# Two edits to a three-part FP32 transformer trunk at once: high and low x in one matmul, and another order of the mixer's steps

## The chip, the cores and the metric

One core of a Trainium2 chip. The metric is the device time of one execution in microseconds (us). The kernel before takes 1033.99 us, the median of three runs (1033.08 to 1035.55). TensorE has two clock levels here, 2.4 GHz (granted clock 1.00 in the profile) and 1.2 GHz (0.50).

## What is computed

Two layers over x of 256 tokens by 1024 features, in FP32. Each layer has a half-step FFN, a mixer of three head groups, and a second half-step FFN, each with a residual and a LayerNorm behind it.

```python
def swiglu(x, w_gate, w_up, w_down):
    return (jax.nn.silu(x @ w_gate) * (x @ w_up)) @ w_down

for l in range(DEPTH):
    x = layer_norm(ALPHA * x + 0.5 * swiglu(x, ffn1_w_gate[l], ffn1_w_up[l], ffn1_w_down[l]), ...)
    x = layer_norm(ALPHA * x + hybrid_mixer(x, ...), ...)
    x = layer_norm(ALPHA * x + 0.5 * swiglu(x, ffn2_w_gate[l], ffn2_w_up[l], ffn2_w_down[l]), ...)
```

The hidden width is 2816. The mixer makes one input product x @ w_in and feeds three groups with it: a gated recurrence (RG-LRU) behind a causal convolution, attention of six heads with a forget gate, and a state-space group (S5) with a GELU and a gate. Their outputs go through a root-mean-square norm each and one output product.

## The kernel before, in words

**Precision.** TensorE takes FP32 in one rounded pass (type fp32r). To keep the precision, every large operand is kept as a high part (rounded) and a low part (what rounding left). A product is three matmuls: high by high, high by low, low by high. `mm3` (lines 1605 to 1609) issues them. For features (`features`, line 1627, and the later `z_event`s) the weights are the stationary operand, in tiles of 128 x 128, and x, transposed, is the moving one, 256 columns. For the down product the moving operand is 512 columns of weights.

**Pieces.** Weights come in 157 pieces of 128 x 2048 through a ring of five slots (`RING`). A piece is loaded by SyncE once the piece five before is used (`pieces_used`), ScalarE copies it to its high part (`split_hi`, line 689), VectorE subtracts for the low part (`split_lo`, line 1072). Each engine's order is written out by hand; `ahead(n)` stands where an engine splits piece n.

**An FFN** (TensorE: `ffn`, line 1748) runs over 11 pairs q of 256 hidden features. A pair has a gate piece, an up piece and a down piece. Pair 0 has the tokens as output rows (`first_pair`), and its product is turned by four transposes. For pairs 1 to 10 TensorE does gate(q), up(q), down(q-1); pass q is this triple. The last three down products come at the end, in halves. Gate goes to PSUM bank 4, up to bank 6, each 512 wide: two tiles of features side by side, 256 tokens each. The down product accumulates in banks 0 to 3 over the whole FFN. Behind a pair stand, in this order: SiLU on ScalarE (`silu_pair`, line 725), the product with up on VectorE (`hidden`, line 1101), the high part on ScalarE (`hidden_hi`, line 730), the low part on VectorE (`hidden_lo`, line 1110). Gate(q) waits for SiLU(q-1), up(q) for the product of q-1. The product of the first pair is taken from banks 4 to 7, its second token tile from banks 4 and 5 (`TOK_BANKS`, `hidden_rows`, line 1086).

**Tables.** Beside the first FFN of a layer the parameters of the mixer are turned and worked out: `turn(parR)`, `outputs_turned` (in the code before part of `ffn`), `inputs_turned`, `responses` on TensorE, with copies on ScalarE and VectorE, and powers on GpSimd (lines 556 to 637). They use banks 5 and 7, which are free of FFN work in the passes.

**The mixer** (VectorE lines 1537 to 1594, ScalarE 960 to 1037, TensorE 1993 to 2050, GpSimd 642 to 672). TensorE's input products are `z_event(0)` to `z_event(17)`. Between them stand the S5 inputs, the forget sums, the S5 outputs (`s5_outputs`, line 1852, waits for VectorE's last rotation, line 1440), the gates of the recurrence, and for each head scores, transposed probabilities and values. A head goes: `scores` (TensorE), `attn_logits` (VectorE), `attn_exp` (ScalarE), `attn_recip` (VectorE), `attn_scale` (GpSimd, line 645), `turn_probs` (TensorE). Between the S5 outputs and the GLU product the S5 result is put from block order into token order: a GELU on ScalarE (`s5_gelu`, line 879) into `gin`, then 16 small copies by VectorE (`blocks_out`, line 1500) into `gs`. TensorE's order around the two edits is

```python
s5_outputs(); gates(1); scores(0); scores(1); z_event(12); gates(2); z_event(13)
turn_probs(0); glu(); scores(2); scores(3); turn_probs(1); z_event(14)
```

Of the kernel before, what the change touches and what calls it, by code (L numbers as in the profile page):

```python
# [106 lines left out]
RG_V_OM = 1  # L107
RG_V_GATED = 7
# [6 lines left out]
def trunk(nc, x, w, out):  # L115
    ctx = ExitStack()
    with ctx:
# [15 lines left out]
        xT_hi = sb("xT_hi", [P, KD, SEQ], F32R)  # L133
        xT_lo = sb("xT_lo", [P, KD, SEQ], F32R)
# [76 lines left out]

        def qpad(h):
            return qf[:, h, :] if h < 4 else qT[:, h - 4, :]
# [37 lines left out]
        hi_done = sem("hi_done")  # L251
        lo_done = sem("lo_done")
# [53 lines left out]
        def used(L, pos):  # L306

            return L * LAYER_N + pos + 1

# [158 lines left out]
        def _(pool):  # L468
# [28 lines left out]
            for L in range(DEPTH):  # L497
# [164 lines left out]

                attn_scale(0)
# [22 lines left out]
        def _(act):  # L686
# [20 lines left out]
            for L in range(DEPTH):  # L707
# [17 lines left out]
                def silu_pair(f, q):  # L725

                    act.wait_ge(pieces_used, used(L, gate_pos(f, q)))
                    A.activation(silu, bank[4][:, :], ACT.Silu).then_inc(ly.silu_done, 1)  # L728
# [13 lines left out]

                def ffn(f):
# [7 lines left out]
                    for q in range(1, PAIRS - 2):  # L751
                        if q == 2 and f == 0:
                            exponentials()
                            outputs_in()
# [3 lines left out]
                        ahead(base + gate_pos(f, q + 1))  # L758
                        ahead(base + up_pos(f, q + 1))
                        hidden_hi(f, q)  # L760
                        if q < PAIRS - 3:
                            ahead(base + down_pos(f, q))
                    silu_pair(f, PAIRS - 2)
                    if f == 0:
                        inputs_in(0)
                    ahead(base + gate_pos(f, PAIRS - 1))
                    ahead(base + up_pos(f, PAIRS - 1))
                    hidden_hi(f, PAIRS - 2)
                    if f == 0:
                        inputs_in(2)  # L770
                    ahead(base + down_pos(f, PAIRS - 3))
                    silu_pair(f, PAIRS - 1)
                    ahead(base + down_pos(f, PAIRS - 2))
                    if f == 0:
                        responses_in()
                    ahead(base + down_pos(f, PAIRS - 1))
                    if f == 0:
                        responses()
# [7 lines left out]
                def outputs_in():  # L786

                    act.wait_ge(c_turned, L + 1)
                    for r in range(2):
                        A.activation(cpow[:, r, :, 0, :], bank[7][:, r * SEQ:(r + 1) * SEQ], ACT.Copy)\  # L790
                            .then_inc(cpow_ready, 1)

                def inputs_in(first):

                    for n in (first, first + 1):
                        act.wait_ge(b_turned, 4 * L + n + 1)
                        A.activation(bst[:, n // 2, 4 * (n % 2):4 * (n % 2) + 4, :], bank[5 + 2 * (n % 2)][:, :], ACT.Copy)\
                            .then_inc(bst_ready, 1)

                def responses_in():  # L800

                    for n in range(2):
                        act.wait_ge(k_summed, 2 * L + n + 1)
                        A.activation(ksb[:, 4 * n:4 * n + 4, :], bank[5 + 2 * n][0:CH, :], ACT.Copy).then_inc(k_evac, 1)
# [186 lines left out]
                ahead_mix(8)  # L991
                attn_exp(0)
                attn_exp(1)
                query_out(12, 1)
# [56 lines left out]
        def _(vec):  # L1051
# [25 lines left out]
            for L in range(DEPTH):  # L1077
# [23 lines left out]
                def hidden(f, q):  # L1101

                    vec.wait_ge(ly.silu_done, silu_count(f, q))
                    vec.wait_ge(pieces_used, used(L, up_pos(f, q)))
                    vec.wait_ge(ly.hid_lo, PAIRS * f + q)
                    if q == 1:
                        vec.wait_ge(ly.hid_turned, f + 1)
                    V.tensor_tensor(hid, silu, bank[6][:, :], ALU.mult).then_inc(ly.hid_done, 1)  # L1108
# [8 lines left out]
                def ffn(f):  # L1117
# [7 lines left out]
                    for q in range(1, PAIRS - 2):  # L1125
                        if q == 1 and f == 0:
                            spread_steps()
                        elif q == 2 and f == 0:
                            angles()
                        ahead(base + gate_pos(f, q + 1))  # L1130
                        ahead(base + up_pos(f, q + 1))
                        hidden(f, q)
                        if q == 2 and f == 0:
                            softplus()
                        hidden_lo(f, q)
                        if q < PAIRS - 3:
# [4 lines left out]
                    ahead(base + up_pos(f, PAIRS - 1))  # L1141
                    hidden(f, PAIRS - 2)
                    hidden_lo(f, PAIRS - 2)
                    ahead(base + down_pos(f, PAIRS - 3))
                    ahead(base + down_pos(f, PAIRS - 2))
                    if f == 0:
                        skip_terms()
# [53 lines left out]
                def angles():  # L1201
# [872 lines left out]
```

## Time and profile before

| | |
|---|---|
| median of three runs | 1033.99 us (1033.08 to 1035.55) |
| profiled execution | 1034.52 us |
| its span, first to last instruction | 1032.8 us |
| TensorE matmuls | busy 97%, 6982 |
| TensorE weight loads | busy 90%, 6982 |
| VectorE | busy 62% |
| ScalarE | busy 48% |
| GpSimd | busy 31% |
| mean granted TensorE clock | 0.983 |
| DMA | 176.68 MB, mean 171 GB/s |

Times in the trace are microseconds from the span's start. A matmul's row shows its start, and its end is modelled: matmuls overlap, so the pace is read from start to start. The square brackets at a row's end give the engine's idle time before it and who ended it.

### The profile page before, as it was taken

How to read it: one execution, taken by the hardware profiler on the slowest of the kernel's cores; microseconds unless marked ns; L12 is line 12 of the kernel's file. 1: busy time of each engine (PE TensorE's matmuls, PEld its weight loads, DVE VectorE, ACT ScalarE, POOL GpSimd, SP SyncE). 2: the span in 40 equal slices, each digit the busy share in tenths (PEclk: the TensorE clock that was granted, in tenths of full speed). 3: DMA queues.
4: the chain of work that ended last, by engine and by line, in shares of the span. 5: the costliest groups of instructions: out<-in, count | busy, mean ns of one | idle time of the engine just before them, and what ended most of it. 6: DMA issues, size and time to landing. Idle time of an engine off the chain costs nothing.

```text
span 1032.8 us, 16441 instructions
## 1 busy us (share of the span) xinstructions
PE 997.9 (97%) x6982; PEld 934.5 (90%) x6982; DVE 639.7 (62%) x756; ACT 493.1 (48%) x602; POOL 320.1 (31%) x382
## 2 busy tenths in 40 slices
PE   7999999999899999999999999999999999999997
PEld 6999999898788999999899999998988889999995
DVE  4674644788687744444787664457787876545446
ACT  4553433647774443433555434264668544343441
POOL 3039991051230700000062699700703334000000
PEclk9999999999899999999999999999979999999998
DMA  9755565374144656565486656545622357555541
GB/s 299 231 193 179 189 189 178 120 195 135 42 134 152 226 182 196 173 202 168 158 234 205 201 168 202 176 151 164 164 82 82 123 171 237 175 193 186 182 164 41
DMA packets 142392, 176.68 MB, mean 171 GB/s; under 512 B 11312, under 2 KB 126704, under 8 KB 142320
## 3 DMA queue, kind: packets, MB, share of 16 engines
q1 hardware_dynamic: 140592, 169.35, 51.7%
q0 software_dynamic: 1728, 6.29, 1.6%
q8 instruction: 55, 0.90, 0.4%
q14 instruction: 17, 0.14, 0.0%
HBM read 174.56 MB, written 1.05 MB: 170 GB/s over the span
## 4 chain that ended last, share of the span: by engine, by line
PE 87%; DVE 8%; ACT 2%; issue 1%; DMA 1%; POOL 1%; SPq 0%; DVEq 0%
PE bank L1607 27%; PE bank L1608 27%; PE bank L1609 27%; PE bank L1612 2%; DVE wlo L1074 1%; DVE gs L1507 1%; ACT u L876 1%; ACT whi L692 1%; PE bank L1742 1%; PE bank L1932 1%; DVE xT_f L1317 1%; PE bank L1860 1%; DMA xtok<-in_x 1%; PE bank L1891 1%; DVE xa L1397 1%
## 5 line engine op out<-in xcount | busy, mean ns | idle before, releaser
L1074 DVE TENSOR_TENSOR wlo<-raw,whi 128x2048 fp32r<-128x2048 f32 (+1 forms) x157 | 387.6, 2490 | 286.8 <-ACT whi L692 286.4
L1607 PE MATMUL bank<-xT_hi,whi 128*128 128x256 f32 x1504 | 429.0, 285 | 0.0
L1609 PE MATMUL bank<-xT_hi,wlo 128*128 128x256 f32 x1504 | 425.6, 283 | 0.0
L1608 PE MATMUL bank<-xT_lo,whi 128*128 128x256 f32 x1504 | 425.6, 283 | 0.0
L692 ACT ACTIVATE whi<-raw 128x2048 fp32r<-128x2048 f32 (+1 forms) x157 | 293.4, 1895 | 12.6 <-DMA raw<-in_ffn_w_up 4.8
L1607 PEld LDWEIGHTS bank<-xT_hi,whi 128*128 128x128 f32 x1504 | 288.5, 192 | 3.4 <-issue 1.7
L1608 PEld LDWEIGHTS bank<-xT_lo,whi 128*128 128x128 f32 x1504 | 288.5, 192 | 1.3
L1609 PEld LDWEIGHTS bank<-xT_hi,wlo 128*128 128x128 f32 x1504 | 288.4, 192 | 0.0
L1607 PE MATMUL bank<-whi,act_hi 128*128 128x512 f32 x376 | 147.6, 393 | 0.0
L1608 PE MATMUL bank<-wlo,act_hi 128*128 128x512 f32 x376 | 146.8, 391 | 0.0
L1609 PE MATMUL bank<-whi,act_lo 128*128 128x512 f32 x376 | 146.5, 390 | 0.0
L527 POOL TENSOR_TENSOR xtok<-xn,lngb 128x1024 f32<-128x1024 f32 x10 | 32.3, 3228 | 336.7 <-DVE xT_lo L1349 336.7
L728 ACT ACTIVATE gs<-bank 128x512 f32<-128x512 f32 x40 | 23.9, 597 | 209.6 <-PE bank L1609 209.5
L740 ACT ACTIVATE act_hi<-uT 128x512 fp32r<-128x512 f32 x36 | 22.8, 632 | 130.4 <-DVE uT L1108 130.4
L1609 PEld LDWEIGHTS bank<-whi,act_lo 128*128 128x128 f32 x376 | 70.6, 188 | 15.1
L1607 PEld LDWEIGHTS bank<-whi,act_hi 128*128 128x128 f32 x376 | 70.8, 188 | 13.7
L1608 PEld LDWEIGHTS bank<-wlo,act_hi 128*128 128x128 f32 x376 | 70.8, 188 | 13.2
L1607 PE MATMUL bank<-whi,xT_hi 128*128 128x256 f32 (+1 forms) x192 | 58.4, 304 | 10.3 <-DVE xT_lo L1349 9.4
L1609 PE MATMUL bank<-whi,xT_lo 128*128 128x256 f32 (+1 forms) x192 | 57.4, 299 | 0.0
L1608 PE MATMUL bank<-wlo,xT_hi 128*128 128x256 f32 (+1 forms) x192 | 57.3, 298 | 0.0
L1607 PEld LDWEIGHTS bank<-whi,xT_hi 128*128 128x128 f32 x192 | 40.3, 210 | 11.7 <-DVE xT_lo L1349 10.3
L1114 DVE TENSOR_TENSOR act_lo<-uT,act_hi 128x512 fp32r<-128x512 f32 x36 | 26.1, 726 | 23.8 <-ACT act_hi L740 23.8
(309 smaller groups left out, 1066.2 us busy)
## 6 DMA issues: line engine op xcount, KB each, us to landing
raw<-in_ffn_w_up SPq DMA_DIRECT2D x44, 1024.0 KB, 5.4
raw<-in_ffn_w_down SPq DMA_DIRECT2D x44, 1024.0 KB, 5.0
raw<-in_ffn_w_gate SPq DMA_DIRECT2D x43, 1024.0 KB, 5.4
raw<-in_w_in SPq DMA_DIRECT2D x12, 1024.0 KB, 5.3
raw<-in_w_out SPq DMA_DIRECT2D x8, 1024.0 KB, 5.4
raw<-in_w_in SPq DMA_DIRECT2D x12, 512.0 KB, 5.3
lngb<-in_ln_g POOLq DMA_DIRECT2D x6, 512.0 KB, 5.8
lngb<-in_ln_b POOLq DMA_DIRECT2D x6, 512.0 KB, 6.8
```

Source lines behind the costliest of these rows:

```text
L527: mark_x(pool.tensor_tensor(xtok[:, t, :], xn[:, t, :], lngb[:, 0, :], ALU.mult))
L692: A.activation(piece(whi, n, 8, PC)[:, :, cols], piece(raw, n, 8, PC)[:, :, cols], ACT.Copy).then_inc(hi_done, 1)
L728: A.activation(silu, bank[4][:, :], ACT.Silu).then_inc(ly.silu_done, 1)
L740: A.activation(hid_tiles(q)[0], src.rearrange("p (a n) -> p a n", a=2), ACT.Copy)\
L876: A.activation(u4[b * CH:(b + 1) * CH, i::4, 1:], src[i * CH:(i + 1) * CH, :, :, b], ACT.Copy)\
L1074: V.tensor_tensor(piece(wlo, n, 8, PC)[:, :, cols], piece(raw, n, 8, PC)[:, :, cols], piece(whi, n, 8, PC)[:, :, cols].bitcast(F32), ALU.s ...
L1114: V.tensor_tensor(lo, src.rearrange("p (a n) -> p a n", a=2), hi.bitcast(F32), ALU.subtract)\
L1317: lnstep(V.tensor_scalar(xT_f[:, 1, k, :], bank[LN_BANKS[n][t][1]][:, k * P:(k + 1) * P], prow(g0, 4 + k), prow(b0, 4 + k), ALU.mult, ALU. ...
L1607: T.matmul(out, a_hi, b_hi, start=first, stop=False)
L1608: T.matmul(out, a_hi, b_lo, start=False, stop=False)
L1609: return T.matmul(out, a_lo, b_hi, start=False, stop=last)
L1612: return T.transpose(dst, src, ident[:, :])
```

## The change

Two edits, put in together.

**x side by side.** `xT_hi` and `xT_lo` become two halves of one tile, `xT[P, KD, 2, SEQ]`. `features` issues, for each of eight row tiles k, one matmul of the high weights with 512 columns (high x and low x) and one of the low weights with high x, 256 columns. Each feature tile gets a bank of its own: gate 4 and 5, up 6 and 7. In a bank, columns 0 to 255 hold high·high + low·high, columns 256 to 511 high·low. ScalarE copies the upper halves to SBUF (`low_part`), VectorE adds the lower halves (`gate_sums`, and at the head of `hidden`), SiLU and the product then work on SBUF. Gate(q) and up(q) wait for these sums of q-1. The table work that used banks 5 and 7 moves to places between passes where gate's banks 4 and 5 are free. `z_event` and `rows` keep three matmuls.

```diff
-        xT_hi = sb("xT_hi", [P, KD, SEQ], F32R)
-        xT_lo = sb("xT_lo", [P, KD, SEQ], F32R)
+        xT = sb("xT", [P, KD, 2, SEQ], F32R)
+        xT_hi, xT_lo = xT[:, :, 0, :], xT[:, :, 1, :]
...
-                def features(n, bnk):
+                def features(n, bnk, second=None):
...
                     for ft in range(2):
+                        if ft and second:
+                            pe.wait_ge(*second)
                         for k in range(KD):
                             c = slice(ft * P, (ft + 1) * P)
-                            ins = mm3(bank[bnk][:, ft * SEQ:(ft + 1) * SEQ], hi[:, k, c], lo[:, k, c],
-                                      xT_hi[:, k, :], xT_lo[:, k, :], k == 0, k == KD - 1)
+                            T.matmul(bank[bnk + ft][:, :], hi[:, k, c], xT[:, k, :, :].rearrange("p a n -> p (a n)"),
+                                     start=k == 0, stop=False)
+                            ins = T.matmul(bank[bnk + ft][:, 0:SEQ], lo[:, k, c], xT_hi[:, k, :], start=False,
+                                           stop=k == KD - 1)
...
+                    if q == 1:
+                        pe.wait_ge(ly.silu_done, silu_count(f, 0))
+                        features(base + gate_pos(f, q), 4, (ly.hid_done, silu_count(f, 0)))
+                    else:
+                        pe.wait_ge(parts_added, gate_sums_done(L, f, q - 1))
+                        features(base + gate_pos(f, q), 4)
...
+                def low_part(f, q, first, dst):
...
+                    A.activation(dst.rearrange("p (a n) -> p a n", a=2), banks[:, first:first + 2, SEQ:], ACT.Copy)\
+                        .then_inc(low_copied, 1)
...
                 def hidden(f, q):
 
+                    both = hid.rearrange("p (a n) -> p a n", a=2)
+                    vec.wait_ge(low_copied, up_sums_done(L, f, q))
+                    V.tensor_tensor(both, banks[:, 6:8, 0:SEQ], both, ALU.add).then_inc(parts_added, 1)
+                    vec.wait_ge(parts_added, up_sums_done(L, f, q))
                     vec.wait_ge(ly.silu_done, silu_count(f, q))
...
+                    V.tensor_tensor(hid, silu, hid, ALU.mult).then_inc(ly.hid_done, 1)
+
+                def gate_sums(f, q):
+
+                    both = silu.rearrange("p (a n) -> p a n", a=2)
+                    vec.wait_ge(low_copied, gate_sums_done(L, f, q))
+                    V.tensor_tensor(both, banks[:, 4:6, 0:SEQ], both, ALU.add).then_inc(parts_added, 1)
```

TensorE's first FFN of a layer: the parameters are turned after gate sum 1 and gate(2) waits until VectorE has copied them (`parameters_in`, behind the product of pass 1); the output tables are turned after up(2), the input tables after up(6) and up(7), the responses after up(8) (`MATS = 6`).

**The mixer's order.**

```diff
@@ GpSimd
+                pool.wait_ge(y_gelu, L + 1)
+                for i in (2, 3):
+                    block_moves(pool, i)
+                pool.wait_ge(ys_gelu, 16 * L + 16)
                 attn_scale(0)
@@ ScalarE
-                ahead_mix(8)
                 attn_exp(0)
                 attn_exp(1)
+                ahead_mix(8)
                 query_out(12, 1)
@@ VectorE
                 ahead_mix(2)
-                ahead_mix(3)
                 forget_log()
                 forget_series()
+                conv(0)
+                ahead_mix(3)
                 s5_turn_back()
-                conv(0)
                 s5_scans()
...
                 ahead_mix(5)
-                blocks_out()
                 attn_logits(0)
                 attn_logits(1)
-                ahead_mix(6)
+                blocks_out()
                 attn_recip(0)
                 attn_recip(1)
-
+                ahead_mix(6)
                 ahead_mix(7)
```

`block_moves(engine, i)` is four of the 16 small copies; VectorE's `blocks_out` keeps i = 0 and 1, GpSimd takes 2 and 3.

## Rows read from the trace of the kernel before

**Rows 1.** The page, busy time, share of the span and instructions.
```profile
PE 997.9 (97%) x6982; PEld 934.5 (90%) x6982; DVE 639.7 (62%) x756; ACT 493.1 (48%) x602; POOL 320.1 (31%) x382
```

**Rows 2.** TensorE's waits: waiter, releaser, us in total, times, longest.
```profile
PE bank L1607 <- DVE xT_lo L1349: 9.4, 5, 2.0
```

**Rows 3.** Timeline, one pass of layer 0's second FFN: start, us, engine, instruction.
```profile
374.95 0.28 PE L1607 MATMUL bank<-xT_hi,whi 128*128 128x256 f32 x1
...
386.46 0.40 PE L1607 MATMUL bank<-whi,act_hi 128*128 128x512 f32 x1
...
391.93 0.28 PE L1607 MATMUL bank<-xT_hi,whi 128*128 128x256 f32 x1
```

**Rows 4.** The same pass: busy us per engine, then SiLU and VectorE's product.
```profile
374.95:391.93 16.98, 16.98 (x122) 16.02 (x120) 8.07 (x6) 6.64 (x5) 0.00 (x0) 1.00 0.58 186
...
380.90 0.60 ACT L728 ACTIVATE gs<-bank 128x512 f32<-128x512 f32 x1 [6.99 <-PE bank L1609]
387.74 0.68 DVE L1108 TENSOR_TENSOR uT<-gs,bank 128x512 f32<-128x512 f32 x1
```

**Rows 5.** Timeline, starts of layer 1's FFNs: gate product 1 and VectorE.
```profile
531.69 0.28 PE L1607 MATMUL bank<-xT_hi,whi 128*128 128x256 f32 x1
534.84 0.41 DVE L1098 TENSOR_TENSOR uT<-gs,bank 128x256 f32<-128x256 f32 x1
...
849.54 0.28 PE L1607 MATMUL bank<-xT_hi,whi 128*128 128x256 f32 x1
853.54 0.41 DVE L1098 TENSOR_TENSOR uT<-gs,bank 128x256 f32<-128x256 f32 x1
```

**Rows 6.** Timeline of TensorE in the mixers of layer 0 and layer 1.
```profile
253.24 0.43 PE L1858 MATMUL bank<-u,kst 128*128 128x64 f32 x2 [1.97 <-DVE xn L1440]
...
272.16 0.90 PE L1612 MATMUL bank<-ident,lngb 128*128 128x128 f32 x3 [4.52 <-POOL lngb L650]
...
278.00 0.36 PE L1607 MATMUL bank<-xT_hi,whi 128*128 128x256 f32 x1
...
760.82 0.43 PE L1858 MATMUL bank<-u,kst 128*128 128x64 f32 x2 [1.97 <-DVE xn L1440]
...
783.33 0.55 PE L1612 MATMUL bank<-ident,lngb 128*128 128x128 f32 x3 [1.54 <-POOL lngb L650]
...
787.00 0.36 PE L1607 MATMUL bank<-xT_hi,whi 128*128 128x256 f32 x1
```

**Rows 7.** Timeline of VectorE, layer 0's mixer: a weight split, the 16 block moves.
```profile
236.74 2.29 DVE L1074 TENSOR_TENSOR wlo<-raw,whi 128x2048 fp32r<-128x2048 f32 x1 [3.84 <-ACT whi L692]
...
260.38 4.88 DVE L1507 COPY gs<-gin 32x128 f32<-32x128 f32 x16
```

**Rows 8.** Timeline of ScalarE, layer 0's mixer.
```profile
234.69 0.21 ACT L969 ACTIVATE fx<-fx 128x12 f32<-128x12 f32 x1
...
258.85 0.60 ACT L882 ACTIVATE gin<-bank 128x512 f32<-128x512 f32 x1 [0.84 <-PE bank L1860]
...
262.19 1.91 ACT L692 ACTIVATE whi<-raw 128x2048 fp32r<-128x2048 f32 x1
...
266.18 0.40 ACT L945 ACTIVATE lngb<-lngb,nmx 128x128 f32<-128x128 f32 x1 [0.77 <-DVE nmx L1520]
...
268.73 0.77 ACT L895 ACTIVATE kpad<-bank 64x256 f32<-64x256 f32 x2
```

**Rows 9.** Timeline of GpSimd, layer 0's mixer: the first head's scaling, the second's first.
```profile
269.26 2.39 POOL L648 TENSOR_SCALAR lngb<-lngb,rrec 128x128 f32<-128x128 f32 x1 [33.31 <-DVE rrec L1524]
271.63 0.47 POOL L650 TENSOR_SCALAR lngb<-lngb,rrec 128x256 f32<-128x256 f32 x1
272.08 0.37 POOL L648 TENSOR_SCALAR lngb<-lngb,rrec 128x128 f32<-128x128 f32 x1
```

**Rows 10.** Busy us of PE, PEld, DVE, ACT, POOL; then clock, DMA share, GB/s.
```profile
334.70:338.00 3.30, 3.30 (x18) 3.30 (x16) 2.58 (x1) 0.93 (x3) 3.22 (x2) 0.50 0.00 0
761.30:775.00 13.70, 13.70 (x59) 13.05 (x58) 9.73 (x19) 7.49 (x10) 0.00 (x0) 0.50 0.15 59
```

More of the change, by code:

```diff
@@ L210, in trunk, with block_moves @@
         qf = xT_f[:, :, :, :].rearrange("p c a n -> p (c a n)").rearrange("p (h n) -> p h n", h=4)
+        def block_moves(engine, i):
+            src = gin[:, 0, :].rearrange("p (q i j) -> p q i j", q=2, i=4)
+            dst = gs[:, :, :].rearrange("p q (j s) -> p q j s", s=BLK)
+            for b in range(BLK):
+                engine.tensor_copy(dst[i * CH:(i + 1) * CH, :, :, b], src[b * CH:(b + 1) * CH, :, i, :]).then_inc(ys_gelu, 1)
         def qpad(h):
@@ L753, in ffn @@
                             exponentials()
-                            outputs_in()
+                        gate_part(f, q)
+                        ahead(base + gate_pos(f, q + 1))
                         silu_pair(f, q)
@@ L1719, in down_rows, with outputs_turned @@
                     return ins
+                def outputs_turned():
+                    pe.wait_ge(ly.tab_step, TAB_C)
+                    pe.wait_ge(parts_added, gate_sums_done(L, 0, 2))
+                    for r in range(2):
+                        for q in range(2):
+                            ins = turn(bank[5][:, (2 * r + q) * P:(2 * r + q + 1) * P],
+                                       cexp[:, q, r, :, :].rearrange("p a b -> p (a b)"))
+                    ins.then_inc(c_turned, 1)
                 def inputs_turned(first):
                     pe.wait_ge(ly.tab_step, TAB_B)
+                    pe.wait_ge(parts_added, gate_sums_done(L, 0, MATS + first // 2))
                     for n in (first, first + 1):
-                        if n == 0:
-                            pe.wait_ge(par_ready, L + 1)
-                        elif n == 1:
-                            pe.wait_ge(cpow_ready, 2 * L + 2)
-                        else:
-                            pe.wait_ge(bst_ready, 4 * L + n - 1)
                         for i in range(4):
-                            ins = turn(bank[5 + 2 * (n % 2)][:, i * P:(i + 1) * P], bpow[:, n // 2, 4 * (n % 2) + i, :])
+                            ins = turn(bank[4 + n % 2][:, i * P:(i + 1) * P], bpow[:, n // 2, 4 * (n % 2) + i, :])
                         ins.then_inc(b_turned, 1)
@@ L1741, in responses @@
                             for r in range(2):
-                                ins = T.matmul(bank[5 + 2 * n][0:CH, (i % 4) * P:(i % 4 + 1) * P],
+                                ins = T.matmul(bank[4 + n][0:CH, (i % 4) * P:(i % 4 + 1) * P],
                                                bpow[:, r, i, (BLK - 1) * CH:],
```

128 lines of the change are left out of this document (76 added, 52 removed).

## The prediction

> **What bounds the kernel now.** I read the page's busy shares first. TensorE is busy 97% of the span, and what ends a chain of waits is its own work [rows 1]. Its list of waits is next: the longest group, 9.4 us, is the five hand-overs after a LayerNorm, where it waits for VectorE's last low part [rows 2]. The change leaves those alone. Then the timeline of one middle pass of an FFN. Products follow each other without a gap: 96 matmuls of 256 columns from 374.95 to 386.46 us, 119.9 ns each, then 24 of 512 columns to 391.93 us, 227.9 ns each [rows 3]. So time comes from two places only: fewer nanoseconds in the dense stream, or the holes of the mixer [rows 6].
>
> **Part 1, high and low x side by side.** Of each three matmuls of 256 columns, two (high weight by high x, high weight by low x) become one of 512. The columns stay 768; a matmul and a weight load go. A pair costs 227.9 + 119.9 = 347.8 ns where three cost 359.7, so 11.9 ns are saved [rows 3]. There are 20 such products in each FFN (the first pair keeps its form), four FFNs and 16 triples in a product: 1280 pairs, **15.2 us**. What the two durations say is that a matmul costs its columns at 2.4 GHz (106.7 and 213.3 ns) and some 13 to 14 ns besides. The Trainium skill, "TensorE: Matmul & The Clock Gate", section "Back-to-back issue gap", gives N/2.4 plus about 2.5 ns for an isolated stream of matmuls; by that a triple would lose 2.5 ns, 3.2 us in all. The rows of this kernel, with a weight load before each matmul, do not agree with 2.5, and the sum goes by the rows.
>
> The join of the two halves is new: ScalarE copies the low half out of PSUM, VectorE adds the high half, for gate and for up; the final product then reads SBUF twice. I price the copy at the SiLU's 0.60 and the add at the old product's 0.68 us [rows 4]. A pass of 16.98 us holds 8.07 us of VectorE and 6.64 of ScalarE [rows 4]; with 1.4 and 1.2 more they are far from full. The gate banks are needed again only after the up product and a down product, 5.7 + 5.5 = 11 us later, and the join takes 1.3 us plus at most two weight splits ahead of it. I cost the join at nothing in the middle passes. At an FFN's end the last down product starts 5.5 us after the last up product (two half down products cover it), and the chain there grows from about 2 to 3.4 us: still covered.
>
> **Where the cover is gone: the start of each FFN.** Gate product 1 now fills bank 5 in its second half, and that bank still holds up rows which VectorE must have multiplied. In layer 1 gate product 1 starts at 531.69 and at 849.54; its first half takes 8 pairs, 2.8 us; VectorE's product ends at 535.25 and 853.95 [rows 5]. Stalls of 0.8 and 1.7 us. Layer 0 has VectorE done in time. The parameters' copy moves behind the up join and gate product 2 waits for it: behind a down product of 5.5 us, I allow 0.4 us in layer 1. Sum of new stalls **+2.9 us**; bounds 0 (VectorE earlier) and 6 (every start like the worst). The transposes and responses of the S5 tables move to passes 2 and 6 to 8, each with a whole down product before their bank is wanted: nothing. GpSimd's tables are the source and were finished long before pass 6.
>
> **Part 2, the mixer.** VectorE idles 3.84 us before a weight split that waits for ScalarE until 236.73, though the exponential that the forget series needs was done at 234.90 [rows 7, 8]. Series and first convolution go ahead of that split, so everything behind comes 1.84 us earlier: TensorE starts the S5 outputs at 251.4 rather than 253.24, and at 758.98 rather than 760.82; the stall of 1.97 us nearly goes [rows 6]. Next late is TensorE itself.
>
> Then the wait of 4.52 us (layer 0) and 1.54 us (layer 1) for GpSimd's scaled probabilities [rows 6]. Today the first exponential starts at 266.18. Logits go ahead of the 16 block moves (4.88 us) [rows 7], half of the moves goes to GpSimd, and ScalarE's split (1.91 us) goes behind the exponentials. ScalarE becomes what is late: its GELU starts at 258.0 rather than 258.85 (table loaded, S5 outputs there), and from there 266.18 - 258.85 - 0.77 idle - 1.91 split = 4.65 us to the first exponential, 262.7 [rows 8]. Two heads end 0.9 and 1.8 us later, and VectorE's reciprocal and GpSimd's two scalings (0.37 and 0.47 when nothing holds them [rows 9]) give the first head at about 264.8. TensorE wants it at 251.4 + (267.64 - 253.24) = 265.8: no stall. The transposes, the GLU product and the next scores take 787.00 - 783.33 = 3.7 us at full clock [rows 6]; the keys those scores need are out at 258.0 + (269.50 - 258.85 - 0.77) = 267.9 [rows 8], just in time. The second head's scaling runs into VectorE's next split, as the first one does today (2.39 us where 0.37 is usual) [rows 9]; I allow 1 us. So the query product behind it starts at 270.4 rather than 278.00, and 778.0 rather than 787.00: 7.6 and 9.0 us [rows 6]. Of layer 1's gain a good part is the clock: it was at 0.50 (1.2 GHz) from 761.3 to 775.0 after the stall, at a cost of 6.8 us [rows 10]; with a stall of 0.1 to 0.4 us instead I take it to stay at 2.4 GHz. ScalarE's chain in the second half of the mixer is dense, so I keep 7.0 and 8.4: **15.4 us**.
>
> The moves on GpSimd are not in this trace. From below: the cost of a scaling of 128 x 128, 0.37 us, times 8 is 3.0 us, done before the reciprocal. From above: each held by a VectorE operation as the 2.39 us scaling was, 19 us, which VectorE's own work (8 moves of 0.3 us, then waits for ScalarE) can't hold up that long; I take 4 us as the end, 1.5 us of it on the path per layer. The skill, "SBUF — State Buffer", section "Who interferes with whom", says that a VectorE operation with two SBUF inputs and a GpSimd one shut each other out for a whole instruction; the 2.39 us agrees. Bounds of part 2: 4 us (only the earlier S5) and 18 us.
>
> **The sum.** The profiled execution took 1034.5 us, 0.5 above the median of the three runs, which is no more than their spread. 1034.5 - 15.2 + 2.9 - 15.4 = 1006.8; against the median 1006.3. I say **1006**.
>
> **Rivals.** (a) The mixer's gain stays small: ScalarE's queue takes the place of the wait, or the clock falls again at another spot. For it: ScalarE has table loads and splits ahead of each exponential [rows 8]; half clock came in layer 1's mixer [rows 10]. Against: both known stalls lose their cause. 4 to 9 us instead of 15.4: about 1015. Chance 0.2. (b) A pair costs what a triple costs, 359.7 ns: the array streams 768 columns either way, and the 13 ns turn out to hang on the switch between high and low weights, of which there are as many as before. Then part 1 gains nothing: 1006.8 + 15.2 = 1022. Against it stand the steady 227.9 ns of 512 columns, where weights change at each matmul [rows 3]. 0.07. By the skill's 2.5 ns, named above, it would be 1019. (c) **Slower.** Bank hand-over: gate q+1 may not start before VectorE's sum of gate q, and that sum stands in VectorE's one queue, with the next weight splits (2.3 us each [rows 7]) and itself behind ScalarE's copy. It decides only if sum and splits end more than 11 us after the product; then each of 72 later products could wait. To be slower it must cost over 28 us, 0.4 us each: 1040. VectorE's 8 us in 17 speak against. 0.04. (d) The half clock after FFN starts (3.3 us long, 1.7 us lost each [rows 10]) comes at fewer places: 996 to 1000. 0.1.
>
> **How the numbers follow.** The forecast (1001 to 1012) has 0.59, and the rest is as above. The range 996 to 1022 takes in (a), (b) and (d) and leaves out (c) and odd cases. 0.2%, 2 us, is about what a measurement of this kernel can tell from no change. Faster 0.95, same 0.01, slower 0.04.
>
> **What would show it.** In the profile after: 512-column feature matmuls some 228 ns apart from the next start, 256-column ones 120; a middle pass of 16.6 us without a gap; new waits of TensorE for VectorE's row product in layer 1's FFN starts; the S5 output stall under 0.5 us; no wait of over 1.5 us for the scaled probabilities; full clock through the mixer of layer 1. I am wrong if middle passes show gaps, if pairs take 360 ns, or if from the start of the S5 outputs to that of the query product behind the second head's transposes (24.8 and 26.2 us now [rows 6]) more than 22 us pass.

## The result, and the profile after

The kernel after takes 1020.06 us, the median of five runs (1019.12 to 1024.93), beside 1033.99 us of the kernel before (1032.96 to 1035.55). The ratio is 0.9869, interval 0.9846 to 0.9891: 13.9 us faster. That is half of the 28 us that the sum gave. The sign and the range held, the size did not.

The profiled execution took 1024.93 us, the slowest of the five; its span is 1023.1 us, 9.7 us under the 1032.8 of before. The other four executions, 1019.12 to 1020.51 us, have no trace, so the stages below explain 9.7 us and not the 13.9. The page of the kernel after, against [rows 1]:

```profile
PE 983.3 (96%) x5702; PEld 858.1 (84%) x5702; DVE 700.4 (68%) x820; ACT 538.8 (53%) x682; POOL 332.3 (32%) x398
```

The 1280 matmuls are gone, and TensorE's busy time fell by 14.6 us, though a busy time of modelled ends says little. The kernel after, TensorE's list of waits (waiter, releaser, us in total, times, longest), against [rows 2]:

```profile
PE bank L1662 <- DVE xT L1409: 9.4, 5, 2.0
PE bank L1667 <- POOL lngb L668: 6.0, 2, 3.1
...
PE bank L1691 <- DVE uT L1144: 3.5, 3, 1.5
PE bank L1931 <- DVE xn L1500: 2.7, 2, 1.4
PE bank L1691 <- DVE par L1261: 2.5, 1, 2.5
```

and the two mixer lines of the same list in the kernel before:

```profile
PE bank L1612 <- POOL lngb L650: 6.1, 2, 4.5
PE bank L1858 <- DVE xn L1440: 3.9, 2, 2.0
```

In the kernel after the first line stands as before. The second is the wait for scaled probabilities, which was to go and still takes 6.0 us, 6.1 before. The third and the fifth are new waits at FFN starts, 6.0 us together. The fourth is the wait before the S5 outputs, 2.7 us where it was 3.9.

**Where the time went, stage by stage.** Stages of the two profiled executions, cut at the starts of down products, before and then after:

| stretch | before | after | difference |
|---|---|---|---|
| start and first FFN, layer 0 | 204.2 | 204.7 | +0.5 |
| mixer, layer 0, to its output product | 91.8 | 89.0 | -2.7 |
| output product, second FFN, layer 0 | 217.1 | 216.8 | -0.3 |
| first FFN, layer 1 | 197.2 | 196.1 | -1.1 |
| mixer, layer 1 | 94.7 | 88.9 | -5.8 |
| output product, second FFN, end | 227.9 | 227.6 | -0.3 |

So in this execution the mixers gave 8.5 us of a forecast 15.4, and the four FFNs 1.2 us of a forecast 12.3. Part of the first row isn't the change: the first down product starts 1.9 us earlier (35.66 us where before had 37.58), and it starts at 35.63 in mix_only too, which has the old x layout.

What the mixers gained is mostly clock. Their two waits above together shortened by 1.3 us. Half clock (granted clock 0.50) lay in the mixers for 6.8 us from 269.8 and 13.7 us from 761.3 before, and after for 3.4 us from 270.4 and 3.4 us from 772.2. That is 13.7 us less of it, worth some 6.8 us, an estimate that takes the stretches as dense. The other executions agree: the mean granted clock was 0.980 to 0.987 in those of the kernel before, 0.978 to 0.985 in x_only, which has the old mixer order, and 0.989 to 0.992 in those of the kernel after.

**A middle pass.** The kernel after, timeline of TensorE in the second FFN of layer 0 (start, us, instruction), against [rows 3]:

```profile
375.76 0.40 PE L1691 MATMUL bank<-xT,whi 128*128 128x512 f32 x1
376.00 0.28 PE L1693 MATMUL bank<-xT,wlo 128*128 128x256 f32 x1
376.12 0.40 PE L1691 MATMUL bank<-xT,whi 128*128 128x512 f32 x1
376.35 0.28 PE L1693 MATMUL bank<-xT,wlo 128*128 128x256 f32 x1
376.47 0.40 PE L1691 MATMUL bank<-xT,whi 128*128 128x512 f32 x1
```

The first two 512-column matmuls start 0.36 us apart, the next two 0.35. The median over the pass is 236 ns behind a 512-column matmul and 117 ns behind a 256-column one. The 32 pairs of the pass take 11.29 us from the first start to that of the down product (374.01 to 385.30), 352.8 ns a pair, where the prediction had 347.8. The down product behind them takes 5.50 us where it took 5.47. The pass is dense and takes 16.79 us (16.98 before, 16.6 forecast), with more work on the two other engines; columns as in [rows 4]:

```profile
374.50:391.30 16.80, 16.80 (x90) 14.31 (x89) 9.56 (x8) 7.76 (x7) 0.00 (x0) 1.00 0.58 188
```

VectorE's 8.07 us became 9.56, ScalarE's 6.64 became 7.76, and TensorE has no gap.

**The FFN starts.** The kernel after, timeline of TensorE at four places: layer 0's second FFN, layer 1's two, and gate product 2 of layer 0's first:

```profile
342.75 0.51 PE L1691 MATMUL bank<-xT,whi 128*128 128x512 f32 x1 [1.46 <-DVE uT L1144]
...
532.82 0.51 PE L1691 MATMUL bank<-xT,whi 128*128 128x512 f32 x1 [0.62 <-DVE uT L1144]
...
844.53 0.51 PE L1691 MATMUL bank<-xT,whi 128*128 128x512 f32 x1 [1.46 <-DVE uT L1144]
...
43.95 0.50 PE L1691 MATMUL bank<-xT,whi 128*128 128x512 f32 x1 [2.55 <-DVE par L1261]
```

What VectorE and GpSimd did ahead of the first of them, from the timeline of the kernel after:

```profile
337.86 4.51 DVE L1120 TENSOR_TENSOR wlo<-raw,whi 128x2048 fp32r<-128x2048 f32 x1 [2.27 <-ACT whi L714]
342.29 0.41 DVE L1144 TENSOR_TENSOR uT<-gs,bank 128x256 f32<-128x256 f32 x1
...
337.83 2.39 POOL L545 TENSOR_TENSOR xtok<-xn,lngb 128x1024 f32<-128x1024 f32 x1
```

and the same split and GpSimd operation in the timeline of the kernel before, not shown until now:

```profile
339.82 2.44 DVE L1074 TENSOR_TENSOR wlo<-raw,whi 128x2048 fp32r<-128x2048 f32 x1 [1.98 <-ACT whi L692]
...
340.05 4.47 POOL L527 TENSOR_TENSOR xtok<-xn,lngb 128x1024 f32<-128x1024 f32 x1
```

The product that TensorE waits for takes 0.41 us, but a weight split stands ahead of it in VectorE's queue. Before, the split began 0.23 us ahead of GpSimd's operation and took 2.44 us, while GpSimd's was held. After, GpSimd began 0.03 us ahead, its operation took 2.39 us, and the split was the one held: 4.51 us. Two operations changed their order by a quarter of a microsecond, and VectorE's product came 2.1 us later.

**The mixer.** The kernel after, timeline of TensorE in both mixers, against [rows 6]:

```profile
252.92 0.43 PE L1931 MATMUL bank<-u,kst 128*128 128x64 f32 x2 [1.36 <-DVE xn L1500]
...
270.42 0.90 PE L1667 MATMUL bank<-ident,lngb 128*128 128x128 f32 x3 [3.10 <-POOL lngb L668]
...
275.76 0.36 PE L1662 MATMUL bank<-xT,whi 128*128 128x256 f32 x1
...
754.89 0.43 PE L1931 MATMUL bank<-u,kst 128*128 128x64 f32 x2 [1.37 <-DVE xn L1500]
...
772.22 0.69 PE L1667 MATMUL bank<-ident,lngb 128*128 128x128 f32 x2 [2.94 <-POOL lngb L668]
...
777.54 0.36 PE L1662 MATMUL bank<-xT,whi 128*128 128x256 f32 x1
```

From the S5 outputs to the query product now pass 22.8 and 22.65 us (24.8 and 26.2 before, 19.0 forecast). The wait of 4.52 us became one of 3.10, and in layer 1 the wait of 1.54 grew to 2.94. Who holds it is seen on GpSimd and VectorE. The kernel after, timeline of GpSimd, against [rows 9]:

```profile
265.44 4.46 POOL L666 TENSOR_SCALAR lngb<-lngb,rrec 128x128 f32<-128x128 f32 x1 [1.72 <-DVE rrec L1580]
```

and of VectorE in the same stretch:

```profile
264.81 0.17 DVE L1580 RECIPROCAL rrec<-rsum 128x2 f32<-128x2 f32 x1
...
265.28 4.47 DVE L1120 TENSOR_TENSOR wlo<-raw,whi 128x2048 fp32r<-128x2048 f32 x2
```

The first head's reciprocal was done at 264.98. GpSimd's scaling started 0.46 us later, and by then VectorE had begun two weight splits in a row. The scaling, 0.37 us when nothing holds it, took 4.46 us and ended some 0.15 us behind the second split (269.90 and 269.75).

### The profile page after: what moved, and what is told of

Its sections match the earlier page's. It is cut to its first block, busy times and chain, and to the rows that moved or that the text cites. A ratio compares the mean times of both kernels' runs of the same rounds, so it can differ in the third digit from the quotient of the medians.

```text
span 1023.1 us, 14125 instructions
## 1 busy us (share of the span) xinstructions
PE 983.3 (96%) x5702; PEld 858.1 (84%) x5702; DVE 700.4 (68%) x820; ACT 538.8 (53%) x682; POOL 332.3 (32%) x398
## 4 chain that ended last, share of the span: by engine, by line
PE 82%; DVE 8%; ACT 3%; issue 2%; SPq 2%; POOL 2%; DMA 1%; DVEq 0%; POOLq 0%
PE bank L1691 28%; PE bank L1693 14%; PE bank L1662 11%; PE bank L1664 11%; PE bank L1663 11%; PE bank L1667 2%; SPq L430 2%; DVE wlo L1120 1%; ACT whi L714 1%; DMA raw<-in_ffn_w_up 1%; ACT u L922 1%; PE bank L1815 1%; POOL lngb L666 1%; PE bank L2005 1%; DVE xT_f L1377 1%
## 5 line engine op out<-in xcount | busy, mean ns | idle before, releaser
L1691 PE MATMUL bank<-xT,whi 128*128 128x512 f32 x1280 | 456.0, 400 | 6.2 <-DVE uT L1144 3.5
L1693 PE MATMUL bank<-xT,wlo 128*128 128x256 f32 x1280 | 360.0, 281 | 0.0
L714 ACT ACTIVATE whi<-raw 128x2048 fp32r<-128x2048 f32 (+1 forms) x157 | 297.2, 1897 | 14.8 <-DMA raw<-in_ffn_w_up 6.1
L1691 PEld LDWEIGHTS bank<-xT,whi 128*128 128x128 f32 x1280 | 241.2, 188 | 67.2 <-DVE uT L1144 4.9
L1693 PEld LDWEIGHTS bank<-xT,wlo 128*128 128x128 f32 x1280 | 242.5, 189 | 1.2
L1160 DVE TENSOR_TENSOR gs<-bank,gs 128x512 f32<-128x512 f32 x40 | 27.6, 691 | 105.7 <-ACT gs L762 105.5
L1662 PEld LDWEIGHTS bank<-whi,act_hi 128*128 128x128 f32 x376 | 70.6, 188 | 15.2 <-issue 0.4
L775 ACT ACTIVATE act_hi<-uT 128x512 fp32r<-128x512 f32 x36 | 22.7, 631 | 84.6 <-DVE uT L1154 84.6
L1662 PE MATMUL bank<-whi,xT 128*128 128x256 f32 (+1 forms) x192 | 56.6, 295 | 10.7 <-DVE xT L1409 9.4
L1662 PE MATMUL bank<-xT,whi 128*128 128x256 f32 x224 | 65.7, 293 | 0.0
L1663 PE MATMUL bank<-xT,whi 128*128 128x256 f32 x224 | 63.3, 283 | 0.0
L1664 PE MATMUL bank<-xT,wlo 128*128 128x256 f32 x224 | 63.3, 283 | 0.0
L1663 PE MATMUL bank<-wlo,xT 128*128 128x256 f32 (+1 forms) x192 | 55.8, 291 | 0.0
L1664 PE MATMUL bank<-whi,xT 128*128 128x256 f32 (+1 forms) x192 | 55.5, 289 | 0.0
```

Source lines behind the costliest of these rows:

```text
L714: A.activation(piece(whi, n, 8, PC)[:, :, cols], piece(raw, n, 8, PC)[:, :, cols], ACT.Copy).then_inc(hi_done, 1)
L775: A.activation(hid_tiles(q)[0], src.rearrange("p (a n) -> p a n", a=2), ACT.Copy)\
L1160: V.tensor_tensor(both, banks[:, 4:6, 0:SEQ], both, ALU.add).then_inc(parts_added, 1)
L1662: T.matmul(out, a_hi, b_hi, start=first, stop=False)
L1663: T.matmul(out, a_hi, b_lo, start=False, stop=False)
L1664: return T.matmul(out, a_lo, b_hi, start=False, stop=last)
```

## The experiments

The differences from the kernel after are of medians taken at different times. The ratios to the kernel before, which ran beside each, give 2.5 us for grouped (the medians 3.8), 6.4 for waitpn (6.9), 2.3 for ffnstart (2.1) and 20.6 for combo (19.9), each give or take 3 us. So grouped and ffnstart alone are not clear of the noise by their time, though each of their executions is faster than every one of the kernel after; for them the traces carry the argument.

**The x layout alone** (run x_only). The kernel after with the old order of the mixer: VectorE's and ScalarE's steps back in their old places, all 16 block moves on VectorE.

```diff
-                for i in (2, 3):
-                    block_moves(pool, i)
...
-                    for i in (0, 1):
+                    for i in range(4):
```

> The changed kernel with the old order in the mixer, so only x side by side. By the stages of the two profiles the mixer gave 2.7 us in layer 0 and 5.8 us in layer 1, the FFNs 1 us in the profiled run. Theory (the two edits are independent): 8.5 us slower than the changed kernel, about 1028.5 us, and the mixer's stretches as long as before. Rival (x side by side shifts the phase of the mixer, and part of its gain is that): under 1025 us.

Measured: 1029.32 us (ten runs, 1026.54 to 1035.1), ratio 0.9971, interval 0.9952 to 0.999. **The layout is worth 3 us by the ratio, 4.5 by the medians**, not the 12.3 of the sum. The time is that of the theory of two independent edits (1028.5). The mixers take 93.4 and 91.2 us in its profile, 184.5 together beside 186.5 before, and their half clock is 13.7 us in layer 0 and 10.2 in layer 1; the row of the first stretch (columns as in [rows 10]):

```profile
251.60:265.30 13.70, 13.70 (x60) 13.07 (x59) 9.61 (x19) 7.40 (x10) 0.00 (x0) 0.50 0.18 71
```

**The mixer's order alone** (run mix_only). The kernel before with nothing but the second edit, the steps of its diff as they stand.

> The kernel before with only the new order in the mixer. Theory (the edits are independent, and GpSimd's lock sets what the mixer can give): the first scaling is held for over 4 us as in the changed kernel, stalls of 3 us before the transposes stay, the half clock of 13.7 us in layer 1 goes; 8 to 10 us faster than before, 1024 to 1026 us. Rival (the mixer alone meets another phase, and the scaling slips in ahead of the splits): stalls under 1 us, 1018 us.

Measured: 1026.12 us (1023.75 to 1027.04), beside 1032.67 of before in the same comparison; ratio 0.9934, interval 0.991 to 0.9958: **6.5 us**, less than the 8 to 10 expected. Its waits for scaled probabilities are 1.9 and 2.8 us. The 13.7 us of half clock left layer 1, but came in layer 0, from 251.3 us. The timeline of its GpSimd shows the same held scaling without any of the new layout:

```profile
268.96 4.14 POOL L655 TENSOR_SCALAR lngb<-lngb,rrec 128x128 f32<-128x128 f32 x1 [3.85 <-DVE rrec L1531]
```

The two parts' ratios multiplied are 0.9905, and both at once have 0.9869 (0.9846 to 0.9891). They are not far from adding up; whether the pair gives 3.7 us more than its parts, these intervals don't settle.

**Grouped by width** (run grouped). Per feature tile first the eight 512-column matmuls, then the eight of 256; same operands, same count.

```diff
                         for k in range(KD):
-                            c = slice(ft * P, (ft + 1) * P)
                             T.matmul(bank[bnk + ft][:, :], hi[:, k, c], xT[:, k, :, :].rearrange("p a n -> p (a n)"),
                                      start=k == 0, stop=False)
+                        for k in range(KD):
                             ins = T.matmul(bank[bnk + ft][:, 0:SEQ], lo[:, k, c], xT_hi[:, k, :], start=False,
                                            stop=k == KD - 1)
```

> Per feature tile first all eight matmuls of 512 columns, then all eight of 256, instead of in turn. Theory (the change of width from matmul to matmul costs the missing 6 ns a pair): 512 columns at 227 to 228 ns from start to start and not 236, 1280 x 6 ns = 7.7 us faster than the changed kernel, about 1012.5 us. Rival (the tile x with both halves, or a bank written in two widths, makes the 512 slower): they stay at 236 ns, 1020 us.

Measured: 1016.3 us (1014.79 to 1018.79), ratio 0.9845 (0.9824 to 0.9866), so 3.8 us less than the kernel after. The run's timeline of TensorE:

```profile
378.97 2.00 PE L1691 MATMUL bank<-xT,whi 128*128 128x512 f32 x8
380.81 1.12 PE L1694 MATMUL bank<-xT,wlo 128*128 128x256 f32 x8
381.76 0.40 PE L1662 MATMUL bank<-whi,act_hi 128*128 128x512 f32 x1
```

Eight of each width take 381.76 - 378.97 = 2.79 us, 348.5 ns a pair; the medians are 228 and 120 ns and the pass is 16.61 us long. That is the pair and the pass of the prediction, within 1 ns and 0.01 us. The rows confirm the pace: 0.18 us less in each of 40 passes are 7.2 us. The medians show half of that, inside the noise named above.

**Both matmuls with 512 columns** (run both512). The low weights go over high and low x too. This adds a low by low product which the three-part product leaves out.

```diff
-                            ins = T.matmul(bank[bnk + ft][:, 0:SEQ], lo[:, k, c], xT_hi[:, k, :], start=False,
-                                           stop=k == KD - 1)
+                            ins = T.matmul(bank[bnk + ft][:, :], lo[:, k, c], xT[:, k, :, :].rearrange("p a n -> p (a n)"),
+                                           start=False, stop=k == KD - 1)
```

> The low weights also go over high and low x, 512 columns, so that all feature matmuls are 512 wide (adds low by low to the low half). Theory (a change of width costs, not the operand): 228 ns each from start to start, a pair 456 ns, 1280 x 102 ns = 131 us slower than the changed kernel, about 1151 us. Rival (the operand x makes 512 columns take 236 ns): 472 ns a pair, 1171 us.

Measured: one execution, 1142.83 us, 123 above the kernel after (131 expected), a pass of 19.95 us. Its timeline of TensorE:

```profile
394.71 0.39 PE L1691 MATMUL bank<-xT,whi 128*128 128x512 f32 x1
394.94 0.39 PE L1693 MATMUL bank<-xT,wlo 128*128 128x512 f32 x1
```

227 ns each. The moving operand across two halves of a tile, the new banks and the change between high and low weights are all still there, at the pace of [rows 3]. Only the change of width at every matmul is gone, and with it that of the width written in the bank; no run parts these two.

**Two and two** (run twos). Two matmuls of 512 columns, then two of 256, in turn.

> Two matmuls of 512 columns, then two of 256, in turn. Theory (each change of width costs): half as many changes, so half of the 6 ns a pair: 351 ns a pair, the first 512 of two at one duration and the second at the other (228 and 236), a middle FFN pass of 16.70 us between the 16.79 of the changed kernel and the 16.61 of the grouped one. Rival (a cost only where widths differ in every neighbour): as grouped, 16.61.

Measured: one execution, 1015.96 us; a pass of 16.59 us, like grouped and not between. Its timeline of TensorE:

```profile
388.75 0.63 PE L1692 MATMUL bank<-xT,whi 128*128 128x512 f32 x2
389.22 0.39 PE L1695 MATMUL bank<-xT,wlo 128*128 128x256 f32 x2
389.45 0.63 PE L1692 MATMUL bank<-xT,whi 128*128 128x512 f32 x2
```

Two of 512 take 0.47 us and two of 256 take 0.23; over a pass that is 348.1 ns a pair. Eight changes of width in a feature tile cost nothing that can be seen, where sixteen cost 4.7 ns a pair. So the cost is not one per change: **of the orders tried, it comes only when the widths alternate one by one**. The theory of a half cost fell. Why one by one is different stays open. Single durations mislead here: the medians in this run are 233 and 115 ns, neither those of grouped (228 and 120) nor those of the kernel after (236 and 117), and only the sum of a pair tells the cost.

**VectorE's splits behind the scaling** (run waitpn). VectorE waits until GpSimd has scaled two heads, and only then begins splits 6 and 7.

```diff
                 attn_recip(1)
+                vec.wait_ge(ly.pn_done, 4)
                 ahead_mix(6)
```

> The changed kernel, but VectorE waits for GpSimd's four scalings of heads 0 and 1 before it starts the two weight splits behind its reciprocals. Theory (the splits keep GpSimd out for 4.5 us): the first scaling takes under 1 us instead of 4.47, TensorE's stalls of 3.3 and 3.1 us before the transposes go, the half clock behind them too; 5 to 9 us faster than the changed kernel, 1011 to 1015 us. Rival (GpSimd is slow there by itself, or ScalarE's keys are the next thing late at once): stalls stay over 2 us or move to the scores, under 2 us gained.

Measured: 1013.15 us (1011.59 to 1014.87), ratio 0.9807 (0.9788 to 0.9825): **6.9 us less than the kernel after**, by one added wait, and inside the 1011 to 1015 expected. Its timeline of GpSimd:

```profile
263.78 0.37 POOL L666 TENSOR_SCALAR lngb<-lngb,rrec 128x128 f32<-128x128 f32 x1 [1.73 <-DVE rrec L1580]
```

and of TensorE, where the transposes follow the product ahead of them with no wait:

```profile
265.39 0.28 PE L1665 MATMUL bank<-xT,wlo 128*128 128x256 f32 x1
265.51 0.49 PE L1668 MATMUL bank<-ident,lngb 128*128 128x128 f32 x3
```

The two mixer stretches went from 89.0 and 88.9 to 84.85 and 84.78 us. Against before they give 6.9 and 9.9 us, 16.8 in all: the 15.4 of the prediction, reached once the splits are out of the way.

**All moves on VectorE** (run waitpn_allvec). As waitpn, without GpSimd's share of the block moves.

```diff
-                for i in (2, 3):
-                    block_moves(pool, i)
...
-                    for i in (0, 1):
+                    for i in range(4):
```

> As the run in which VectorE waits for the scalings, but all 16 block moves stay on VectorE. Theory (with the splits out of the way, the share on GpSimd is worth what VectorE saves before its reciprocals): 8 moves of 0.36 us more, reciprocals 1.5 to 2.5 us later, a stall of 1.5 to 2 us in each layer before the transposes, 3 to 5 us slower than that run, about 1017 us. Rival (ScalarE's exponentials end last anyway): the same 1013 us.

Measured: 1020.9 us (1020.51 to 1024.77), ratio 0.9885 (0.9864 to 0.9906), 7.8 us above waitpn. So GpSimd's half of the moves is a part of the gain, and more of it than I had thought. The first transposes wait 0.36 and 0.34 us only; the larger loss is one step on, at the third head, in the run's timeline of TensorE

```profile
278.65 0.55 PE L1664 MATMUL bank<-ident,lngb 128*128 128x128 f32 x3 [2.23 <-POOL lngb L668]
```

with half clock behind it (6.8 us in layer 0, 3.4 in layer 1). GpSimd's timeline there (two squares, 3.16 us together, end just before it), and VectorE's:

```profile
276.23 1.92 POOL L666 TENSOR_SCALAR lngb<-lngb,rrec 128x128 f32<-128x128 f32 x1
...
276.16 0.96 DVE L1510 SCALAR_TENSOR_TENSOR rgbuf<-mixbuf,rgbuf 128x768 f32<-128x768 f32 x1 [0.82 <-ACT mixbuf L1049]
277.04 0.95 DVE L1514 TENSOR_TENSOR rgbuf<-rgbuf,xa 128x768 f32<-128x768 f32 x1
```

The third head's scaling stood behind the two squares and took 1.92 us itself, where one that nothing holds takes 0.37: again for as long as two VectorE operations in a row. In waitpn the same scaling starts 0.85 us earlier, at 275.38, ahead of these two, and takes 0.37.

**The FFN starts mended** (run ffnstart). VectorE's short operations go ahead of the splits.

```diff
-                    ahead(base + up_pos(f, 1))
...
+                    ahead(base + up_pos(f, 1))
...
-                        ahead(base + up_pos(f, q + 1))
-                        hidden(f, q)
...
+                        ahead(base + up_pos(f, q + 1))
+                        hidden(f, q)
```

The row product of the first pair now comes before the split of up piece 1, and the parameters' copy before that of up piece 2.

> The changed kernel with two steps of VectorE earlier: the first pair's second row product ahead of the split of up piece 1, and the copy of the parameters ahead of the split of up piece 2. Theory (bank 5 and the parameters' copy are held up by a split in front of them in VectorE's queue): the waits in front of the second half of gate product 1 (1.6, 0.8 and 1.6 us) fall under 0.3 us, the one of 2.5 us before gate product 2 of layer 0 goes with its half clock, 4 to 7 us faster, about 1015 us. Rival (the split that comes later is wanted as soon): up product 1 waits instead, under 2 us gained.

Measured: 1017.92 us (1017.14 to 1018.46), ratio 0.9847 (0.9832 to 0.9863), 2.1 us less than the kernel after where 4 to 7 were expected. All of the waits for VectorE's row product and for the parameters have left TensorE's list; the wait for GpSimd, which this edit leaves alone, is the same as before it:

```profile
PE bank L1667 <- POOL lngb L668: 6.0, 2, 3.1
```

In the profile the start of the first FFN is 4.2 us shorter (21.4 to 17.2 us between its first two down products), two others 1.5 us (32.16 to 30.69 and 30.71 us), but that of layer 1's first FFN is 0.9 longer (31.34 to 32.26): half clock fell there, from 518.2 us. The two profiled spans differ by 6.9 us (1023.1 and 1016.2), the medians by 2.1. The kernel after was profiled in its slowest execution, so how much of the 6.0 us of waits its others had isn't known.

**All three mends together** (run combo). Grouped, waitpn and ffnstart in one.

> All three together on the changed kernel: 512-column matmuls grouped, VectorE's splits behind GpSimd's scalings, and in the FFN starts VectorE takes the row product and the parameters' copy before a weight split. The parts act on different stretches, so the theory adds them: 4 to 8 us for the grouping, 7 for the wait, 5 for the starts, about 1003 us. Rival (TensorE closer to its feed waits elsewhere, for splits or pieces): over 1008 us, with new waits for split pieces in the profile.

Measured: **1000.16 us** (997.44 to 1000.76), ratio 0.967 (0.9652 to 0.9688). This beats both kernels, before by 33 us and after by 20. The single gains add up to 3.8 + 6.9 + 2.1 = 12.8 us; together they give 19.9. TensorE's list of waits in this run:

```profile
PE bank L1663 <- DVE xT L1409: 9.4, 5, 2.0
PE bank L1668 <- DMA xtok<-in_x: 5.3, 2, 4.6
PE bank L1668 <- DVE xn L1368: 1.1, 2, 0.5
PE bank L1933 <- DVE xn L1500: 1.1, 2, 0.5
```

Neither GpSimd's scaling nor an FFN start is in it. Half clock came at three places (211.1, 702.6 and 811.8 us, 3.4 us each) where the kernel after had five, not counting the one at the very end, when TensorE has no work left; the mean granted clock is 0.994 beside 0.989. The two profiled spans differ by 24.3 us, and what the traces show adds up to that: 7.2 for the pace, 12.0 for the waits for scalings and at FFN starts, 1.6 for the S5 outputs, some 3.4 for two places of half clock, 24.2 together. That the medians give 7 us more than the three single gains isn't shown to be a gain of its own: the same median of the kernel after stands in all three differences, and 2 us more in it would close 4 of the 7.

## Why the prediction was right and wrong

**Right.** The sign, and that the time fell into the stated range. The join of the halves costs nothing in middle passes: no gap in a pass, and VectorE and ScalarE far from full. The bank hand-over, rival (c), never bound. New waits appeared in both FFN starts of layer 1, where they were named. The 13.7 us of half clock in layer 1's mixer [rows 10] are gone in the profile of after: the window from 758 to 771 us shows 1.00. But full clock through that mixer, one of the signs named, did not come: 3.4 us of half clock follow from 772.2 us, behind the stall of 2.94. The first exponential started at 263.30 in layer 0 where 262.7 was worked out, and GpSimd's eight moves were done 4.5 us after they began (4 forecast). By its own test, more than 22 us from the S5 outputs to the query product, the prediction was wrong on the mixer: 22.8 and 22.65 us passed.

**Wrong, 1: "A pair costs 227.9 + 119.9 = 347.8 ns where three cost 359.7, so 11.9 ns are saved".** Both durations came from streams of one width, and the new order has the widths in turn. There a pair costs 352.8 ns, and the down products behind lose 0.03 us each; a pass went from 16.98 to 16.79 us, and 40 passes give 7.6 us for 15.2. The runs grouped and twos show that the pace of the prediction holds for the same operands as soon as the widths don't alternate one by one, and both512 that 512 columns of this x keep 227 ns. Rival (b) had named a switch as the cost, but that between high and low weights, and both512 excludes it: it keeps this switch and has 227 ns. The Trainium skill ("TensorE: Matmul & The Clock Gate", section "Back-to-back issue gap") has N/2.4 plus about 2.5 ns for an isolated matmul. These rows don't agree: streams of one width stand 13 to 15 ns over their columns, and the alternating ones 22.7 (512) and 10.3 (256).

**Wrong, 2: "The second head's scaling runs into VectorE's next split ... I allow 1 us".** It was the first head's, and it ran into two splits. I worked out when the reciprocal would be done (264.8; it was 264.98) and then took the scaling at its free duration. But in the same diff the split of piece 6 had moved from ahead of the reciprocals to right behind them, next to that of piece 7, and GpSimd begins about 0.5 us after its release. So the new order put 4.5 us of VectorE's work exactly on the scaling. The 22.8 us from S5 outputs to query product exceed the forecast of 19.0 by 3.8. Of these 3.1 are the stall, and the rest, 0.7 us, is the size of the half clock behind the stall (3.4 us, 1.7 lost) less the 1 us allowed. The run waitpn takes nothing but this away and gives back 6.9 us by the medians. The Trainium skill says in "SBUF — State Buffer", section "Who interferes with whom", that such a pair of operations shut each other out for a whole instruction; the row of 4.46 us agrees, and goes further: two instructions in a row.

**Wrong, 3: "so everything behind comes 1.84 us earlier".** It came 0.8 us earlier: from the down product at 204.16 us to the S5 outputs were 49.08 us, after 252.92 - 204.65 = 48.27. VectorE's timeline in the kernel after shows the first operation of the series:

```profile
235.45 1.02 DVE L1225 TENSOR_SCALAR fx<-fx 128x12 f32<-128x12 f32 x1 [2.05 <-ACT fx L1015]
```

It has 12 columns, the next ones of that size take 0.17 us, and GpSimd cleared a tile of 1024 columns at that time (235.50, 0.95 us). The other runs bear this out. In mix_only it is so in layer 0 and not in layer 1; its timelines of VectorE and TensorE:

```profile
233.04 1.01 DVE L1179 TENSOR_SCALAR fx<-fx 128x12 f32<-128x12 f32 x1 [2.07 <-ACT fx L980]
...
741.84 0.17 DVE L1179 TENSOR_SCALAR fx<-fx 128x12 f32<-128x12 f32 x1 [3.60 <-ACT fx L980]
...
250.75 0.43 PE L1865 MATMUL bank<-u,kst 128*128 128x64 f32 x2 [1.63 <-DVE xn L1451]
...
758.46 0.32 PE L1865 MATMUL bank<-u,kst 128*128 128x64 f32 x1 [0.53 <-DVE xn L1451]
```

The new mixer order ran in nine kernels of two layers each. In seven of the 18 mixers this operation ran beside the clear and took 1.0 us, and there TensorE waited 1.36 to 1.63 us for the S5 outputs. In the other eleven it took 0.17 us, and the wait was 0.51 to 0.54. So 0.85 of the 1.03 us that are missing is this one held operation.

**Wrong, 4: "Sum of new stalls +2.9 us".** 0.8 and 1.7 us for layer 1 came out at 0.62 and 1.46. But layer 0, "has VectorE done in time", had 1.46, by the split that came second to GpSimd's operation, and the parameters, "I allow 0.4 us", had 2.55 us in layer 0, with half clock for 3.4 us behind it. By the list of waits it is 6.0 us. The run ffnstart removes them; it gains 2.1 us by the medians and 6.9 between the two profiled spans.

Of the rivals, (a) came nearest for the mixer (a held operation where a wait had been) and half of (b) was true for the layout. All misses were of one kind, a smaller gain, so they add. By the profiled executions they are 7.6 us for the pair, 3.1 for the starts (6.0 for 2.9) and 6.9 for the mixers (8.5 for 15.4, the third miss among them), 17.6 of the 18.1 us between 1006.8 and 1024.9. The median lies 4.9 us lower, and no trace shows where. In the run combo the first, second and fourth miss are mended and the third does not occur (0.17 us in both layers); it takes 1000.2 us, 6 under the forecast, with half clock at three places as rival (d) had it.

## What to carry to other kernels

Take a duration from a stream of the same pattern, not only of the same shape: two widths one by one cost 4.7 ns a pair more than each alone, and issuing them in groups of two or of eight gave it back. When a step is moved, write down beside each short GpSimd operation on the path what VectorE will do in the microsecond after its release; a split there holds it to the split's end, and a wait that delays VectorE gained 6.9 us here. After a wait is removed, look at the short operations behind long splits in the same queue before the next wait is costed. Read the granted clock beside the waits: between the two profiled executions the new mixer order hardly shortened the waits, and most of its gain was half clock that did not come. And look where the profiled execution lies among the others before its stages are used for a median.

## What the runs showed of the hardware that was not expected

- Matmuls of 512 and 256 columns in turn take 352.8 ns a pair; by twos or by eights 348 ns; 512 columns alone 227 to 228 ns.
- A GpSimd operation of 0.37 us took 4.46 us while VectorE ran two splits back to back: between the two splits it did not get in. The same came with two operations of 768 columns (1.92 us for 0.37, in waitpn_allvec).
- The reverse holds too: a VectorE operation of 0.17 us took 1.02 us beside a GpSimd clear of 0.95 us (in seven mixers of 18), and a split of 2.44 us took 4.51 us where GpSimd had begun 0.03 us ahead of it.
- TensorE's granted clock fell to 0.50 for 3.4 to 13.7 us after stalls (of 1.63 us in mix_only, of 2.94 in the kernel after), but not after each (1.46 us at 342.75), and at different places in different runs: 13.7 us in layer 1's mixer before, in layer 0's in x_only and mix_only (x_only has 10.2 us in layer 1's besides), 3.4 us in each in the kernel after. A window of the kernel after, behind the stall of 2.94 us:

```profile
772.20:775.60 3.40, 3.38 (x10) 2.84 (x11) 0.00 (x0) 2.41 (x4) 0.77 (x2) 0.50 0.38 155
```

  So what a removed stall is worth can't be read off its own length alone: in ffnstart the start of one FFN lost its stall of 0.62 us and became 0.9 us longer, with half clock in it.
